# First attention on unscaled rows: turned as they land, RMS roots at read-out, first weight slab in halves on GpSimd

## The chip, the cores and the metric

The kernel runs on one core of a Trainium2 chip, in one launch. The metric is the device time of that core in microseconds (us), the median of repeated runs of the whole kernel; lower is better. The engines are named as the profile names them: PE (TensorE, matrix products; PEld is its weight load), DVE (VectorE), ACT (ScalarE), POOL (GpSimd) and SP (SyncE, which only issues transfers here).

## The reference

A sequence of 256 positions with model width 1024, batch 1, in float32, passes through two transformer blocks and then a third with another design. Only the first attention matters for the change:

```python
h = rms_norm(x, g[0])                 # x * rsqrt(mean(x*x) + EPS) * g
qkv = (h @ w_qkv)                     # 1024 -> 3 * 1024
q = q * NA_HEAD_DIM ** -0.5           # 16 heads of 64
# every position sees all 4 rows of the 4 x 64 grid, 16 columns wide, with a bias table rpb
a = softmax(q k^T + bias)
m = (a v) @ w_o
x = x + rms_norm(m, g[1])
f = conv_glu_ffn(rms_norm(x, g[2]), ...)   # and so on: FFN, gated projection, second attention ...
```

The root rsqrt(mean(x*x) + EPS) is one number per position. It multiplies a whole row of `h`, and therefore a whole row of `h @ w_qkv`; it can be put in before the product or behind it.

## The kernel before

The phases run in the order of `PHASES`: first attention (`na`), FFN, gated projection, second attention, FFN, gated projection, then the last block. Each engine has one hand-written program; the programs meet through semaphores only, so the order of calls in each program is the order of the work.

**Exact products in three passes.** Every float32 operand is split into a high part (rounded to the PE's fast format) and a low part (the operand minus its high part). A product is three matmuls: high by high, high by low, low by high (`product3`). For weights this is a pipeline over slabs of 1 MB (128 x 2048): SP's transfer into `raw` (3 buffers; slab n is issued once the low part of slab n-3 is done), ACT's `feed` copies the high part into `w_hi` (L693), DVE's `feed` subtracts for `w_lo` (L1261), PE waits in `slab(n)` for the low part. For activations `tile_parts` does the same in 8 steps per half of the positions: ACT writes `hT_hi` (L712), DVE `hT_lo` (L1283), and the two take turns.

**The start.** SP issues x in two halves of 128 positions, then slabs 0, 1 and 2. ACT sums the squares of x (`pre(0, t)`, L709), POOL turns them into roots (`powers`, L562 and L567), DVE multiplies x by them (`normed`, L1300), PE transposes the scaled rows (`turn_x`, L2003), and ACT and DVE split them. POOL makes the high part of slab 0 in one cast (L588), DVE its low part. `keep_busy` issues matmuls with no use between these steps. DVE also computes the rotary angles and the lambda sums (`lambdas`, `rotary`, L1873 to L1897) once, after slab 1. Then PE computes the first four column tiles of q and k: `first_columns` for tiles 0 and 1 (high weights against both parts, L2115, then low weights, L2120), `half_columns` for tiles 2 and 3; `turn_taps` transposes small constants (L2022 to L2028).

**The first attention.** 16 column tiles c0 to c15 (128 columns of q or k each), four value pieces, eight units of two heads. Results of PE go through four PSUM banks (`WORK = 4`) in the fixed order of `BANK_ORDER`; group g may be opened only when group g-4 has been read out (`open_bank`, `evacuated`). The order begins

```python
"c0 c1 c2 c3 taps v0.0 v0.1 T0 c4 V0 T1 c5 V1 c6 c7 v1.0 v1.1 T2 V2 T3 c8 V3 ..."   # T takes two banks
```

so c5 goes into the bank that c4 leaves. ACT reads the column tiles out (`columns_out`, L838) into `qT` and `kT`, and the values (`values_out`). The DVE's program around c4 is

```python
expand(3); feed(b + 6); feed(b + 7); output(0); output(1); feed(b + 8); feed(b + 9)
```

where feed(b+6) and feed(b+7) are the low parts of slabs 5 and 6. ACT's is `values_out(0, 0, 0)`, `values_out(0, 0, 1)`, `feed(b + 7)` (high parts of slabs 5 and 6), `columns_out(0, 4)`. PE's is value rows, `half_columns(0, 4)`, `unit_values(0, 0)`, `unit_turn(0, 1)`, `half_columns(0, 5)`.

## Time and profile before

| | us |
|---|---|
| median of 3 runs (lowest, highest) | 1225.22 (1225.15, 1225.36) |
| span of the profiled execution | 1226.3 |
| PE busy | 1210.3 (99%) |
| DVE busy | 945.3 (77%) |
| ACT busy | 672.6 (55%) |
| POOL busy | 138.0 (11%) |
| DMA | 214.52 MB, mean 175 GB/s |

The profiled execution is 1.1 us longer than the median of the unprofiled runs; differences are worked out inside the profile and then set against the median. A busy share says how long an engine had something in it, not that it worked at its peak. The chain that ended last is followed back from the last instruction to whatever released each step, so it names the engine that set the time at each moment.

### The profile page before, as it was taken

To read this page: it belongs to the slowest core of one execution; us is meant where nothing else is said; L and a number is where in the kernel's file an instruction comes from. 1 tells how busy PE (TensorE), PEld (TensorE's weight loads), DVE (VectorE), ACT (ScalarE), POOL (GpSimd) and SP (SyncE) were. 2 spreads that over 40 slices of the span, in tenths; PEclk is the share of its full clock that TensorE was granted. 3 is DMA by queue.
4 is the path that set the end of the run, shared out by engine and by line. 5 is a ranking of instruction groups with operands and counts; after the bars stand their busy time and mean duration, and the time that the engine had idled before them with its cause. 6 is when DMAs were issued, how large, how long until landed. Compare 5 with 4: busy or idle time off the path is not lost.

```text
span 1226.3 us, 17906 instructions
## 1 busy us (share of the span) xinstructions
PE 1210.3 (99%) x6995; PEld 1054.3 (86%) x6995; DVE 945.3 (77%) x1270; ACT 672.6 (55%) x1064; POOL 138.0 (11%) x257
## 2 busy tenths in 40 slices
PE   8999999999999999999999999999999999999997
PEld 7899888888879988888888988888896888888886
DVE  6757699888876588998888898776775778667665
ACT  6656644444575777444446845444675555443435
POOL 4000330000120012000002100000208420000002
PEclk9999999999999999999999999999999999999999
DMA  8834376565445445665554576555455136665540
GB/s 265 245 126 153 105 248 212 185 206 194 151 155 172 138 149 178 213 205 177 178 198 160 188 229 198 187 181 178 146 172 172 36 114 222 206 199 180 199 144 35
DMA packets 149015, 214.52 MB, mean 175 GB/s; under 512 B 4410, under 2 KB 114428, under 8 KB 148932
## 3 DMA queue, kind: packets, MB, share of 16 engines
q1 hardware_dynamic: 145596, 205.39, 51.0%
q0 software_dynamic: 1632, 4.71, 1.5%
q10 hardware_dynamic: 1704, 3.28, 0.8%
q8 instruction: 56, 0.92, 0.3%
q14 instruction: 27, 0.22, 0.1%
HBM read 212.30 MB, written 1.06 MB: 174 GB/s over the span
## 4 chain that ended last, share of the span: by engine, by line
PE 90%; DVE 5%; ACT 2%; DMA 1%; issue 1%; POOL 0%; POOLq 0%; ACTq 0%; DVEq 0%
PE work L2347 24%; PE work L2350 12%; PE acc L1946 10%; PE acc L1947 10%; PE acc L1948 10%; PE work L1946 5%; PE work L1947 5%; PE work L1948 5%; DVE w_lo L1261 2%; PE work L2156 2%; PE work L1968 2%; PE acc L2132 1%; PE work L2336 1%; PE work L2324 1%; PE work L2338 1%; PE work L2461 1%
## 5 line engine op out<-in xcount | busy, mean ns | idle before, releaser
L1261 DVE TENSOR_TENSOR w_lo<-raw,w_hi 128x2048 fp32r<-128x2048 f32 (+1 forms) x194 | 440.4, 2277 | 47.9 <-ACT w_hi L693 47.9
L693 ACT ACTIVATE w_hi<-raw 128x2048 fp32r<-128x2048 f32 (+2 forms) x193 | 365.2, 1899 | 69.3 <-PE work L2350 59.2
L2347 PE MATMUL work<-hT_both,w_hi 128*128 128x512 f32 x1280 | 318.8, 391 | 0.0
L2347 PEld LDWEIGHTS work<-hT_both,w_hi 128*128 128x128 f32 x1280 | 234.8, 188 | 45.1
L2350 PEld LDWEIGHTS work<-hT_both,w_lo 128*128 128x128 f32 x1280 | 174.6, 190 | 12.5
L2350 PE MATMUL work<-hT_both,w_lo 128*128 128x256 f32 x1280 | 178.5, 282 | 0.0
L1946 PE MATMUL acc<-w_hi,aux_hi 128*128 128x512 f32 x400 | 157.9, 395 | 0.0
L1947 PE MATMUL acc<-w_lo,aux_hi 128*128 128x512 f32 x400 | 156.7, 392 | 0.0
L1948 PE MATMUL acc<-w_hi,aux_lo 128*128 128x512 f32 x400 | 155.8, 390 | 0.0
L1048 ACT ACTIVATE aux_hi<-Z 128x256 fp32r<-128x256 f32 x88 | 36.9, 419 | 195.1 <-DVE Z L1671 107.1
L1642 DVE TENSOR_REDUCE Z<-work 128x256 f32<-128x512 f32 x88 | 60.6, 689 | 89.6 <-PE work L2350 87.8
L1948 PEld LDWEIGHTS acc<-w_hi,aux_lo 128*128 128x128 f32 x400 | 75.1, 188 | 16.4
L1946 PEld LDWEIGHTS acc<-w_hi,aux_hi 128*128 128x128 f32 x400 | 75.4, 189 | 13.8 <-issue 0.3
L1947 PEld LDWEIGHTS acc<-w_lo,aux_hi 128*128 128x128 f32 x400 | 75.5, 189 | 12.1
L562 POOL TENSOR_SCALAR ms<-ssq 128x1 f32<-128x1 f32 x26 | 19.3, 744 | 551.3 <-ACT xn L709 444.8
L1946 PE MATMUL work<-hT_both,w_hi 128*128 128x256 f32 x272 | 78.6, 289 | 0.0
L1947 PE MATMUL work<-hT_both,w_hi 128*128 128x256 f32 x272 | 76.9, 283 | 0.0
L1948 PE MATMUL work<-hT_both,w_lo 128*128 128x256 f32 x272 | 76.9, 283 | 0.0
L838 ACT ACTIVATE Z<-work 128x512 f32<-128x512 f32 (+1 forms) x92 | 45.4, 515 | 47.3 <-PE work L1948 35.9
L1946 PE MATMUL acc<-w_hi,hT_both 128*128 128x512 f32 (+1 forms) x184 | 67.8, 368 | 0.6 <-DVE hT_both L1283 0.6
L1948 PE MATMUL acc<-w_hi,hT_both 128*128 128x512 f32 (+1 forms) x184 | 66.7, 362 | 0.0
L1947 PE MATMUL acc<-w_lo,hT_both 128*128 128x512 f32 (+1 forms) x184 | 66.6, 362 | 0.0
(262 smaller groups left out, 1815.4 us busy)
## 6 DMA issues: line engine op xcount, KB each, us to landing
raw<-in_ffn_w_in SPq DMA_DIRECT2D x44, 1024.0 KB, 5.1
raw<-in_ffn_w_out SPq DMA_DIRECT2D x22, 1024.0 KB, 5.1
raw<-in_w_gate SPq DMA_DIRECT2D x22, 1024.0 KB, 5.4
raw<-in_w_up SPq DMA_DIRECT2D x22, 1024.0 KB, 5.3
raw<-in_w_down SPq DMA_DIRECT2D x22, 1024.0 KB, 5.0
raw<-in_na_w_qkv SPq DMA_DIRECT2D x12, 1024.0 KB, 7.5
raw<-in_da_w_qkv SPq DMA_DIRECT2D x12, 1024.0 KB, 5.1
raw<-in_ple_w_gate SPq DMA_DIRECT2D x8, 1024.0 KB, 5.1
```

The costliest lines, as they stand in the source:

```text
L693: act.activation(w_hi[:, n % RING, 0:size], raw[:, n % RAW, 0:size], ACT.Copy).then_inc(hi_done, 1)
L838: act.activation(dst, src, func).then_inc(bank_free[g % WORK], 1)
L1048: act.activation(aux_hi[:, c % 2, :], hid32[:, c % 2, :], ACT.Copy).then_inc(hid_hi_done, 1)
L1261: dve.tensor_tensor(w_lo[:, n % RING, 0:size], raw[:, n % RAW, 0:size], w_hi[:, n % RING, 0:size].bitcast(F32), ALU.subtract).then_inc(lo_ ...
L1642: dve.tensor_reduce(src, bank(g).rearrange("p (e s) -> p s e", e=2), AX.X, ALU.add)\
L1946: pe.matmul(dst, stationary[0], moving[0], start=first, stop=False)
L1947: pe.matmul(dst, stationary[0], moving[1], start=False, stop=False)
L1948: return pe.matmul(dst, stationary[1], moving[0], start=False, stop=last)
L1968: ins = pe.transpose(b[0:width, i * P:i * P + rows], v, ident[0:rows, 0:rows])
L2156: ins = pe.matmul(b[:, (2 * j + a) * n:(2 * j + a + 1) * n], wt[:, cols(2 * k + a)], vtok[:, k, c0:c0 + n], start=k == 0, stop=k == 1)
L2347: pe.matmul(b.rearrange("p (e s) -> p e s", e=2), v[0][:, k, cols(c % 2)], hT_both[:, k, :, :], start=k == 0, stop=False)
L2350: ins = pe.matmul(b[:, 0:S], v[1][:, k, cols(c % 2)], hT_hi[:, k, :], start=False, stop=k == KT - 1)
```

## The change

Before, the rows of x were scaled by their roots ahead of the transposition. After it, the raw rows are transposed as they land, the split and the products of the first attention run on unscaled rows, and the roots come in when PE's results are read. For that they are needed as a row across the free dimension for q and k, which are transposed: PE transposes the roots (`turn_scales(0)`), ACT copies them to `rb0`, and DVE multiplies each column tile with it (`column_scaled`). The values have positions on the partitions, and ACT scales them on the way out. All 16 column read-outs move from ACT to DVE. Slab 0 comes in two transfers, and POOL makes its high and its low part by halves; DVE has nothing more to do with slab 0. The roots are computed behind that on POOL, and behind the transfer of the bias table (`load_rpb`). Rotary work goes ahead of slab 1's low part on DVE. `first_columns` now takes slabs 0 and 1, with high weights for both tiles first. `turn_taps` goes ahead of the first scores, and fewer matmuls keep PE busy. The copy of `gb` is issued later.

```diff
-UNSCALED = [1, 4, 6, 7, 8]
+UNSCALED = [0, 1, 4, 6, 7, 8]
+SCALED_OUT = [1, 4]
         def turned_block(ph, t, step):
+            if ph == 0:
+                return acc[:, step // 4 * 2 + step % 2, step % 4 // 2 * P:(step % 4 // 2 + 1) * P]
+                if n == 0:
+                    sp.dma_start(dst[:, 0:4, :], src[:, 0:4, :]).then_inc(first_half, 16)
+                    sp.dma_start(dst[:, 4:8, :], src[:, 4:8, :]).then_inc(landed[0], 16)
             late_rows(pool)
-            powers("pre0.1")
-            pool.wait_ge(landed[0], 16)
-            pool.tensor_copy(w_hi[:, 0, :], raw[:, 0, :]).then_inc(hi_done, 1)
             for i in range(32):
                 ins = pool.memset(invf[:, i:i + 1], ...)
-            pool.wait_ge(hi_done, 2)
+            pool.wait_ge(first_half, 16)
+            pool.tensor_copy(w_hi[:, 0, first], raw[:, 0, first]).then_inc(first_hi, 1)
+            pool.wait_ge(landed[0], 16)
+            pool.tensor_copy(w_hi[:, 0, second], raw[:, 0, second]).then_inc(hi_done, 1)
+            pool.tensor_tensor(w_lo[:, 0, first], raw[:, 0, first], w_hi[:, 0, first].bitcast(F32), ALU.subtract)
+            pool.tensor_tensor(w_lo[:, 0, second], raw[:, 0, second], w_hi[:, 0, second].bitcast(F32), ALU.subtract)\
+                .then_inc(lo_done, 1)
             load_rpb(0)
+            powers("pre0.1")
@@ ACT, start
-            for t in range(T):
-                pre(0, t)
-            gains(w["norm_g"][0, 1], D)
+            pre(0, 0, (0,))
             evacuated(act, G["vec"])
             tile_parts(0, 0)
             tile_parts(0, 1)
+            pre(0, 0, (1,))
+            pre(0, 1)
             act.wait_ge(hi_done, 1)
             fed[0] = 1
             feed(3)
-            columns_out(0, 0)
-            columns_out(0, 1)
+            scales_out(0)
@@ ACT, attention0: every columns_out(0, n) is gone; values_out has scale=rstd; gains before feed(b + 11)
@@ DVE
+            def column_scaled(n):
+                g, f = G[f"c0.{n}"], n // 4 * 2 + n % 2
+                if n == 0:
+                    dve.wait_ge(scales_ready, UNSCALED.index(0) + 1)
+                full(dve, g)
+                src, roots = [v.rearrange("p (t c) -> p t c", t=T) for v in (bank(g)[:, 0:S], rb0)]
+                dst = (kT if n // 2 % 2 else qT)[:, f, :].rearrange("p (t c) -> p t c", t=T)
+                dve.tensor_tensor(dst if n // 2 % 2 else backwards(dst), src, roots, ALU.mult)\
+                    .then_inc(bank_free[g % WORK], 1)
             def attention0():
                 b = B[0]
+                column_scaled(0)
+                column_scaled(1)
                 feed(b + 3)
+                column_scaled(2)
+                column_scaled(3)
+                taps_out()
                 expand(0)
                 scores(0, 0)
                 expand(1)
-                taps_out()
                 feed(b + 4)
...
                 feed(b + 6)
                 feed(b + 7)
+                column_scaled(4)
                 output(0)
+                feed(b + 8)
+                column_scaled(5)
                 output(1)
-                feed(b + 8)
                 feed(b + 9)
+                column_scaled(6)
+                column_scaled(7)
...
@@ DVE, start
-            tile_parts(0, 0, range(4))
-            normed(0, 1)
-            tile_parts(0, 0, range(4, 8))
+            tile_parts(0, 0)
             tile_parts(0, 1)
-            feed(2)
             lambdas()
             rotary()
+            dve.wait_ge(lo_done, 1)
+            fed[0] = 1
+            feed(2)
@@ PE
+            def first_columns(n):
...
+                for k in range(KT):
+                    if n == 0:
+                        split_done(pe, 0, 1, k)
+                        if k == 0:
+                            pe.wait_ge(first_hi, 1)
+                        if k == 4:
+                            pe.wait_ge(hi_done, 1)
+                    for c in range(2):
+                        pe.matmul(b[c], hi[:, k, cols(c)], hT_hi[:, k, :], start=k == 0, stop=False)
+                        pe.matmul(b[c], hi[:, k, cols(c)], hT_lo[:, k, :], start=False, stop=False)
...
             def attention0():
-                first_columns()
-                half_columns(0, 2)
-                half_columns(0, 3)
+                first_columns(0)
+                turn_scales(0)
+                first_columns(1)
+                turn_taps()
                 unit_scores(0, 0)
-                turn_taps()
-            keep_busy(10)
+            keep_busy(2)
             pe.wait_ge(first_row, 16)
             turn(G["vec"], [vrow[0:KT, :]])
-            keep_busy(5)
+            keep_busy(4)
             turn_x(0, 0)
-            keep_busy(8)
                         turn_x(0, 1)
-                        keep_busy(2)
+                        keep_busy(6)
                         attention0()
```

## Rows read from the trace of the kernel before

**Rows 1.** The page: busy time and instructions of each engine.

```profile
PE 1210.3 (99%) x6995; PEld 1054.3 (86%) x6995; DVE 945.3 (77%) x1270; ACT 672.6 (55%) x1064; POOL 138.0 (11%) x257
```

**Rows 2.** Windows; columns: stretch, length, PE, PEld, DVE, ACT, POOL busy, PEclk, DMA.

```profile
27.30:40.00 12.70, 12.68 (x67) 9.93 (x68) 11.79 (x17) 7.93 (x19) 0.00 (x0) 1.00 0.78 249
```

**Rows 3.** The chain that ended last, first 28 us: start, length, what.

```profile
0.80 3.64 DMA x<-in_x
...
14.56 0.38 ACT hT_both L712
...
15.35 0.38 ACT hT_both L712
...
16.36 4.40 DVE w_lo L1261 x2
```

**Rows 4.** Timeline of PE, 1.5 to 29.1 us: start, length, engine, line, operation.

```profile
1.58 4.38 PE L2015 MATMUL work<-ident 128*128 128x128 f32 x20 [1.58 <-POOL ident L544]
5.89 0.22 PE L1968 MATMUL work<-ident,Z 8*128 8x8 f32 x1
6.04 1.38 PE L2015 MATMUL work<-ident 128*128 128x128 f32 x10
...
18.66 2.13 PE L2120 MATMUL work<-hT_both,w_lo 128*128 128x256 f32 x16
...
26.55 0.28 PE L1948 MATMUL work<-hT_both,w_lo 128*128 128x256 f32 x1
27.32 0.49 PE L2132 MATMUL acc<-Z 64*128 64x256 f32 x2 [0.50 <-ACT Z L838]
```

**Rows 5.** Timeline of POOL, first 20 us, and POOL's subtraction elsewhere, by line.

```profile
9.61 1.89 POOL L588 CAST w_hi<-raw 128x2048 fp32r<-128x2048 f32 x1 [0.99 <-DMA raw<-in_na_w_qkv]
...
18.08 1.51 POOL L579 DMA_DIRECT2D Z<-in_na_rpb  x2 [5.31 <-ACT w_hi L693]
...
L644 POOL TENSOR_TENSOR Z<-Z x7: 1893/1935/2016, 920.3 to 970.8; 128x1024 f32<-128x1024 f32 x6, 128x512 f32<-128x512 f32 x1
```

**Rows 6.** Timeline of POOL after 300 us: a root alone, and one beside DVE.

```profile
323.06 2.35 POOL L565 TENSOR_SCALAR ms<-ssq 128x1 f32<-128x1 f32 x1 [154.85 <-ACT Z L709]
...
341.19 0.22 POOL L562 TENSOR_SCALAR ms<-ssq 128x1 f32<-128x1 f32 x1
...
341.88 0.57 POOL L567 TENSOR_TENSOR rstd<-ms,mhalf 128x1 f32<-128x1 f32 x1
```

**Rows 7.** DVE: the scaling of x by its line (min/median/max ns), then timeline lines.

```profile
L1300 DVE TENSOR_SCALAR xn<-x,rstd x4: 474/484/1725, 6.9 to 11.7; 128x512 f32<-128x512 f32 x4
...
9.79 0.35 DVE L1283 SCALAR_TENSOR_TENSOR hT_both<-acc,vecT,hT_both 128x128 fp32r<-128x128 f32 x1
10.05 1.73 DVE L1300 TENSOR_SCALAR xn<-x,rstd 128x512 f32<-128x512 f32 x1
...
20.67 0.32 DVE L1873 TENSOR_TENSOR Z<-Z 128x128 f32<-128x128 f32 x1
...
24.96 2.29 DVE L1261 TENSOR_TENSOR w_lo<-raw,w_hi 128x2048 fp32r<-128x2048 f32 x1
...
27.97 0.96 DVE L1448 TENSOR_TENSOR Z<-Z 128x768 f32<-128x768 f32 x1 [0.72 <-DMA Z<-in_na_rpb]
...
320.87 4.49 DVE L1261 TENSOR_TENSOR w_lo<-raw,w_hi 128x2048 fp32r<-128x2048 f32 x2
```

**Rows 8.** Around column tile 4: timelines of ACT and DVE, and PE's chain.

```profile
42.46 0.60 ACT L838 ACTIVATE Z<-work 128x512 f32<-128x512 f32 x1 [0.90 <-PE work L1948]
42.95 3.70 ACT L693 ACTIVATE w_hi<-raw 128x2048 fp32r<-128x2048 f32 x2
...
44.89 4.50 DVE L1261 TENSOR_TENSOR w_lo<-raw,w_hi 128x2048 fp32r<-128x2048 f32 x2 [2.96 <-ACT w_hi L693]
49.51 0.42 DVE L1488 TENSOR_TENSOR xn<-work,rinv 128x256 f32<-128x256 f32 x1
...
47.91 0.12 PE work L1946
```

## What the change should do, worked out before it ran

> **What bounds the kernel now.** I read the page first: PE is busy for 1210.3 us [rows 1] of the span of 1226.3. So what counts is the 16 us that PE lacks, and, at the start, the time in which it is only kept busy. The windows say where that ends: from 27.3 us on PE is full (12.68 of 12.70 us) [rows 2]. The change only touches what comes ahead of that and the queues of the first attention, up to some 125 us. The chain gives the order of the start [rows 3]: x lands at 4.44; the splits run in pairs, 14.56 to 15.35, so 0.79 us for two steps, to 16.36; then come the low parts of slabs 0 and 1, 4.40. In between, from 10.05, DVE scaled the second half of x, the first piece in 1.73 us [rows 7]. PE's own timeline [rows 4] has the low products of slab 0 at 18.66, tiles 2 and 3 behind them, from 20.8 until the last starts at 26.55 (48 matmuls, 5.87 us, 0.122 each) and the first scores at 27.32. With 1.06 for eight score matmuls and 0.7 for the taps behind them, the value products start at 29.1. That moment is what I carry: everything behind it is packed, so its shift is the gain, unless a new hole appears later.
>
> **The change: the start.** *Removed*: four scalings of x, the root from the path to the split, DVE's 2.2 us for slab 0. *The split* now starts when the gains and the first four raw blocks are turned. The gains' row is in by 5.89 at the latest, because PE turned it then, only just out of its filler [rows 4]; how much earlier, no row tells, but x itself lands at 4.44 [rows 3]. With four fillers (8 records at 0.12 to 0.22 each, 1.0 to 1.7 us) and four blocks (0.5 to 0.9) the first split stands between 6 and 8.5; I take 6.8, nearer the early end since x's transfer, 128 times larger, took only 3.6. Sixteen splits at 0.395 and a tail of 0.3 end at 13.4, against 16.36. *Slab 0 on POOL*: it lands at 9.55 (the cast started at 9.61 behind it), and the cast of 2048 columns took 1.89, so a half 0.95 [rows 5]; the first half is done before, the second at 10.6. Two subtractions of 1024 columns at 1.94 each [rows 5] end at 14.5, against some 18.5 on DVE. PE's high products keep step with the splits (four matmuls, 0.49, per step of 0.395) and end near 14; the 16 low ones take 2.1 [rows 4] and end near 16.7, against 20.8. That looks like 4 us, but PE then waits for the roots.
>
> **Roots are next in line.** On POOL, behind slab 0, come the two issues of the bias table, 1.5 us [rows 5], so 16.0. A root with all its sums there takes 1.26 (from 341.19 to 342.45) [rows 6], two take 2.6: 18.6. ACT's squares are no later: the splits end for ACT at 13.1, three squares at 0.66 end at 15.1. ACT then makes the high parts of slabs 1 and 2, 1.9 each, until 18.9; DVE does 4.3 us of lambdas and rotary (20.67 to 24.96 [rows 7]) from 13.4 or, if it has to stand behind POOL's second subtraction, from 14.5, so until 17.7 to 18.8, then the low part of slab 1, 2.28, until at most 21.1. So PE: two small transposes, 0.3, to 18.9; tiles 2 and 3, 5.87, to 24.8 (the low part of slab 1 is wanted at 22.8 and there); taps 0.7 to 25.5; scores 1.06 to 26.6. The taps ahead of the scores cover the read-out of tile 3 (0.35). Values start at 26.6 against 29.1: **2.5 us earlier**.
>
> **What must keep up.** The bias table landed just under 27.97, from an issue at 18.08 [rows 5, 7]: 9.9 us. Issued at 14.5 it lands near 24.4, and DVE wants it at 26.2: hidden with 1.8 to spare. Slab 3 is issued with it and its low part is done at about 32.9, against a need at 33.1: a slack of some 0.3, as before. The late `gb`, the sums, `values_out` with a scale and the split transfer I cost at nothing: ACT drops 16 read-outs of 0.37 and has room, and SP is idle from 11 to 18 us; were that cover gone, an issue is 0.4.
>
> **The first attention: a new hole.** Sixteen read-outs go to DVE. The nearest row is its product of a 128x256 PSUM tile, 0.42 [rows 8]; I take 0.35 each as the next instruction starts 0.34 later, 5.6 us together. The place matters more than the sum. Tile 5 uses tile 4's bank. PE opened the bank at 47.91 without a wait, since ACT had read tile 4 right behind its high parts of slabs 5 and 6, which end at 46.65 [rows 8]. Now DVE reads it behind the low parts of slabs 5 and 6, and these hang on ACT's high parts, which start when the second value piece, full at 42.42, has been read. Counted from there all of it moves with PE: subtractions until +7.0 (44.89 + 4.50), tile 4 read at +7.3, PE wants the bank at +5.5. So PE stands still for **1.8 us** (1.7 to 1.9), once. The other places hold: tile 5 is read at +10.7, its bank wanted at +17; tile 8 at 80.8 against 85.6; tile 12 at 94.4 against 100.9; tile 14 at 101.1 against 105.4 (before's clock, in all of them the next value comes from the same kind of count). DVE's seventh scores come 0.7 later, with 2 us before anybody needs them.
>
> **Sum.** -2.5 + 1.8 = -0.7 inside the profile (1226.3 to 1225.6); from the median 1225.22 this gives 1224.6.
>
> **A rule against the trace.** DVE's scaling of x, 0.48 in the median, took 1.73 beside POOL's cast [rows 5, 7], while a split from PSUM beside the same cast kept its 0.35 [rows 7]. And a one-column instruction of POOL took 2.35 at 323.06, where DVE was in its low part until 325.3 [rows 6, 7]. The Trainium skill (SBUF — State Buffer, section on SBUF's two separate sides) says that DVE and GpSimd share one port pair, which a DVE instruction with two SBUF inputs holds against a GpSimd instruction that reads SBUF, for its whole length. The trace agrees in these places. By that rule the splits from PSUM don't suffer from POOL's subtractions, but lambdas and rotary must stand behind the second one.
>
> **Rivals.**
> 1. *The root behind DVE's low part (slower).* If DVE starts slab 1's low part before POOL has started its last power, at 18.0, POOL waits for 2.3 us as in rows 6. Then the roots come at 20.9, values start only 0.2 us early, and with the hole the sum is +1.6: 1226.8. Its point: DVE must be through with rotary before 18.0. For: splits done at 13.4 plus 4.3 is 17.7. Against: POOL's subtraction until 14.5 stops DVE first, as it was stopped at 10.05, and gives 18.8. This is a matter of tenths.
> 2. *No hole at tile 5.* If PE reaches tile 5 later than I count, or DVE's part ends early, 2.5 us stay: 1222.7. Against: the order is fixed in both programs, and all terms are rows.
> 3. *PE at half speed.* Its first 20 records come 0.22 apart, the ten from 6.04 on 0.13 [rows 4], as 1.2 against 2.4 GHz, though the granted clock reads 1.00. It had been busy for 4 us without a pause. The new start is filled less. If it is slow at 10.7, four matmuls take 0.86 a step and the first products end between 17.5 and 19.5: up to 0.9 late, 1225.5; if it falls back in the wait of 2 us for the roots, tiles 2 and 3 lose 1.5 more: up to 1227.
> 4. *Roots not late.* Should POOL be quicker than the rows of other shapes say, by 0.5 per subtraction, it is 1223.6.
>
> **How the numbers follow.** Forecast, the sum as it stands: 45% (1223.9 to 1225.6). Rival 1: 25%. Rival 2: 10%. Rival 3: 12%. Rival 4: 8%. The likeliest gives 1224.6. Two tenths of a per cent, which is about what a measurement of this kernel can tell from no change, are 2.45 us, so faster means under 1222.8, slower over 1227.7. Under 1222.8 is rival 2 in half of its cases and a sum of 4 with good luck: 9%. Over 1227.7 are rivals 1 and 3 together, or a slab that comes late in the thin slack of 0.3: 11%. Same: 80%. The range runs from rival 2's 1222.7 to rivals 1 and 3 with half of their extras, 1227.5.
>
> **What would show it.** In the profile after: the first split near 6.8 and the last near 13.4; POOL's subtractions 1.9 each, low part of slab 0 by 14.5; the second root near 18.6 with no POOL instruction of over 2 us (rival 1 has one, beside a 2.3 us subtraction on DVE); tiles 2 and 3 from 19 to 24.8 at 0.122 a matmul (rival 3: over 0.2); value products from 26.6; one wait of PE of 1.8 us ahead of tile 5, released by DVE's read-out of tile 4, and no other up to 125 us. I would be wrong if POOL's work on slab 0 runs much slower beside DVE's splits, or if the bias table or slab 3 lands later than the same distance behind its issue.

## The result: 8 us slower

The median went from 1225.36 us (1225.15 to 1225.55, five runs) to 1233.37 (1232.10 to 1233.57, five runs). The ratio is 1.0063, with a 95% interval of 1.0053 to 1.0074. The forecast was 1224.6, and the measured time lies outside the range up to 1227.5.

The profile page of the changed kernel, busy time and instructions of each engine, and the granted clock in 40 slices:

```profile
span 1231.6 us, 17868 instructions
PE 1209.7 (98%) x6971; PEld 1054.1 (86%) x6971; DVE 949.7 (77%) x1281; ACT 668.6 (54%) x1049; POOL 144.8 (12%) x260
PEclk8999999999999999999999999999999999999999
```

PE's busy time is 0.6 us less than in [rows 1], while the span is 5.3 us longer: PE does not do more, it waits more. (The span in [rows 1] is that of an execution that was itself some 2.7 us longer than the usual one: executions of 1225.3 us have a span of 1223.6, and the 1.1 us in the text on the kernel before sets a span against a time. Where most of them arise comes below.)

**Where the time arises.** A mark that both kernels have is PE's transposition of x ahead of each later phase. First the kernel before, then the changed one: count, min/median/max in ns, first and last start.

```profile
L2003 PE MATMUL acc<-ident,x x80: 270/272/329, 137.8 to 1007.6; 128*128 128x128 f32 x80
...
L2003 PE MATMUL acc<-ident,x x16: 272/272/273, 872.4 to 878.2; 128*128 128x128 f32 x16
```

```profile
L2048 PE MATMUL acc<-ident,x x80: 270/272/328, 145.5 to 1013.0; 128*128 128x128 f32 x80
...
L2048 PE MATMUL acc<-ident,x x16: 270/272/273, 880.0 to 885.9; 128*128 128x128 f32 x16
```

The first of these marks is 7.7 us later, the one at 880 is 7.6 later, the last 5.4. So all of the loss arises ahead of 138 us, in the start and the first attention, and nothing is won or lost for 730 us behind it. The 2.2 us that seem to come back at the end belong to the profiled execution of the kernel before. Windows, columns as in [rows 2], before and then changed:

```profile
940.00:1000.00 60.00, 58.57 (x355) 50.74 (x356) 44.01 (x63) 29.80 (x57) 22.80 (x18) 0.97 0.21 63
```

```profile
940.00:1000.00 60.00, 58.22 (x361) 49.61 (x360) 42.70 (x65) 32.22 (x67) 29.35 (x25) 1.00 0.22 71
```

The clock of 0.97 over 60 us is a stretch of some 3.4 us at half clock, in that one execution, which costs at most 1.7 us; a wait of PE for ACT in the same stretch is 1.2 us instead of 0.7. Together these are the 2.2 us. So the marks, not the spans, give the effect.

**The start.** POOL's timeline of the changed kernel, with three of DVE's lines among it, the last its low part of slab 1 (start, length, engine, line, operation, idle time before it and its releaser):

```profile
9.96 1.04 POOL L599 CAST w_hi<-raw 128x1024 fp32r<-128x1024 f32 x1 [3.60 <-DMA raw<-in_na_w_qkv]
...
12.18 1.04 POOL L601 CAST w_hi<-raw 128x1024 fp32r<-128x1024 f32 x1 [1.18 <-DMA raw<-in_na_w_qkv]
...
13.19 2.44 POOL L603 TENSOR_TENSOR w_lo<-raw,w_hi 128x1024 fp32r<-128x1024 f32 x1
...
13.60 2.06 DVE L1915 CAST posf<-posi 128x2 f32<-128x2 int32 x1
...
15.59 2.38 POOL L605 TENSOR_TENSOR w_lo<-raw,w_hi 128x1024 fp32r<-128x1024 f32 x1
...
15.69 2.98 DVE L1918 TENSOR_SCALAR Z<-Z,posf 128x32 f32<-128x32 f32 x4
...
17.92 1.47 POOL L587 DMA_DIRECT2D Z<-in_na_rpb  x2
...
21.18 2.48 POOL L570 TENSOR_SCALAR ms<-ssq,ms 128x1 f32<-128x1 f32 x1
21.31 2.28 DVE L1272 TENSOR_TENSOR w_lo<-raw,w_hi 128x2048 fp32r<-128x2048 f32 x1
23.75 0.56 POOL L575 TENSOR_TENSOR rstd<-ms,mhalf 128x1 f32<-128x1 f32 x1
```

Both halves of slab 0 land late (9.9 and 12.1; in [rows 5] the whole slab was there at 9.6), each subtraction takes 2.4, and the second root's sum is stretched from some 0.3 to 2.48 by DVE's subtraction beside it. Then PE:

```profile
24.36 0.48 PE L2055 MATMUL acc<-ident,rstd 128*128 128x128 f32 x1 [3.20 <-POOL rstd L575]
...
28.05 0.41 PE L2165 MATMUL work<-hT_both,w_hi 128*128 128x256 f32 x1
...
30.20 0.28 PE L2166 MATMUL work<-hT_both,w_hi 128*128 128x256 f32 x1
...
30.80 2.08 PE L2170 MATMUL work<-hT_both,w_lo 128*128 128x256 f32 x16
...
33.14 1.19 PE L2181 MATMUL acc<-Z 64*128 64x256 f32 x8
```

It stands for 3.2 us for the root, and the matmuls behind that are 0.41 long, and 0.213 apart, until 29.8, when they go back to 0.28 and 0.12 apart. The windows give the granted clock (the third column from the end, 1.00 being 2.4 GHz): 0.51 between 25 and 30 us is the 1.2 GHz level. It fell while PE stood still, 1.00 from 22 to 23 us and 0.55 from 23 to 24.

```profile
20.00:25.00 5.00, 1.17 (x6) 0.77 (x6) 3.46 (x6) 0.12 (x1) 4.35 (x8) 0.81 1.05 308
25.00:30.00 5.00, 5.00 (x26) 5.00 (x25) 2.95 (x3) 4.94 (x6) 3.89 (x8) 0.51 1.06 268
```

The first scores start at 33.14 against 27.32 [rows 4], the value products at 34.3 against 29.1: 5.2 of the 7.7 us. **Tile 5** adds the next piece; ACT, DVE and PE around it, the lines that answer to [rows 8]:

```profile
48.24 3.70 ACT L708 ACTIVATE w_hi<-raw 128x2048 fp32r<-128x2048 f32 x2
...
50.17 4.49 DVE L1272 TENSOR_TENSOR w_lo<-raw,w_hi 128x2048 fp32r<-128x2048 f32 x2 [2.96 <-ACT w_hi L708]
54.59 0.41 DVE L1530 TENSOR_TENSOR Z<-work,pts 128x256 f32<-128x256 f32 x1
...
55.15 0.36 PE L1982 MATMUL work<-hT_both,w_hi 128*128 128x256 f32 x1 [2.05 <-DVE Z L1530]
```

PE waits for 2.05 us, and tile 5 starts at 55.15 against 47.91 [rows 8], 7.24 later (5.2 + 2.05). The last 0.45 us up to the first mark come from small gaps behind it.

### The profile page after: what moved, and what is told of

It reads as the page before. It is cut to its first block, busy times and chain, and to the rows that moved or that the text cites. A ratio compares the mean times of both kernels' runs of the same rounds, so it can differ in the third digit from the quotient of the medians.

```text
span 1231.6 us, 17868 instructions
## 1 busy us (share of the span) xinstructions
PE 1209.7 (98%) x6971; PEld 1054.1 (86%) x6971; DVE 949.7 (77%) x1281; ACT 668.6 (54%) x1049; POOL 144.8 (12%) x260
## 4 chain that ended last, share of the span: by engine, by line
PE 90%; DVE 4%; ACT 2%; DMA 1%; POOL 1%; issue 1%; SPq 0%; POOLq 0%; ACTq 0%; DVEq 0%
PE work L2396 24%; PE work L2399 12%; PE acc L1982 10%; PE acc L1983 10%; PE acc L1984 9%; PE work L1982 5%; PE work L1983 4%; PE work L1984 4%; DVE w_lo L1272 2%; PE work L2205 2%; PE work L2004 1%; PE acc L2181 1%; PE work L2385 1%; PE work L2373 1%; PE work L2387 1%; PE work L2510 1%
## 5 line engine op out<-in xcount | busy, mean ns | idle before, releaser
L1272 DVE TENSOR_TENSOR w_lo<-raw,w_hi 128x2048 fp32r<-128x2048 f32 (+2 forms) x193 | 438.0, 2275 | 46.7 <-ACT w_hi L708 46.6
L2399 PEld LDWEIGHTS work<-hT_both,w_lo 128*128 128x128 f32 x1280 | 174.6, 190 | 12.5
L2399 PE MATMUL work<-hT_both,w_lo 128*128 128x256 f32 x1280 | 178.5, 282 | 0.0
L1679 DVE TENSOR_REDUCE Z<-work 128x256 f32<-128x512 f32 x88 | 60.6, 688 | 90.6 <-PE work L2399 88.8
L1983 PEld LDWEIGHTS acc<-w_lo,aux_hi 128*128 128x128 f32 x400 | 75.5, 189 | 12.1
L1982 PE MATMUL work<-hT_both,w_hi 128*128 128x256 f32 x256 | 74.0, 289 | 2.1 <-DVE Z L1530 2.1
L1983 PE MATMUL work<-hT_both,w_hi 128*128 128x256 f32 x256 | 72.4, 283 | 0.0
L1984 PE MATMUL work<-hT_both,w_lo 128*128 128x256 f32 x256 | 72.3, 283 | 0.0
L1704 DVE TENSOR_REDUCE Z<-work 128x256 f32<-128x512 f32 x88 | 60.1, 683 | 2.8 <-PE work L2399 2.8
```

The source lines that it names most:

```text
L1272: dve.tensor_tensor(w_lo[:, n % RING, 0:size], raw[:, n % RAW, 0:size], w_hi[:, n % RING, 0:size].bitcast(F32), ALU.subtract).then_inc(lo_ ...
L1679: dve.tensor_reduce(src, bank(g).rearrange("p (e s) -> p s e", e=2), AX.X, ALU.add)\
L1704: dve.tensor_reduce(hid, bank(g + 1).rearrange("p (e s) -> p s e", e=2), AX.X, ALU.add)\
L1982: pe.matmul(dst, stationary[0], moving[0], start=first, stop=False)
L1983: pe.matmul(dst, stationary[0], moving[1], start=False, stop=False)
L1984: return pe.matmul(dst, stationary[1], moving[0], start=False, stop=last)
```

## The experiments

The kernels that ran together share their runs of the kernel before (median 1225.25 beside the first four, 1225.38 beside the next four, 1225.71 beside the two after that, 1225.33 beside the last two). Brackets hold the 95% interval of the ratio. The last four kernels ran on another chip than the first eight, so each is to be compared with the kernel before of its own group.

### One suspect at a time

**Tile 4 read ahead of the second slab.** Is the wait at tile 5 worth its 2 us?

```diff
@@ DVE, attention0
                 feed(b + 6)
-                feed(b + 7)
                 column_scaled(4)
+                feed(b + 7)
                 output(0)
```

> The changed kernel with DVE's read-out of column tile 4 put between the low parts of slabs 5 and 6 instead of behind both. Theory H (the hole at tile 5 is a cost of its own): PE's wait of 2.05 us ahead of tile 5 goes, since the read-out comes 2.2 us sooner, and the time falls by 1.9 to 2.1, from 1233.4 to about 1231.4. Rival (the time is set further on by slabs that land late, so a wait removed here comes back at tiles 6 to 8): the wait at tile 5 goes, another of 1 us or more appears before 80 us, and the time falls by under 1.0.

Measured: 1233.18 us, ratio 1.0061 [1.0046, 1.0076]: 0.2 less than the changed kernel. The wait at tile 5 is gone, but another of the same length stands ahead of the third unit's scores (PE's waits: in total, times, longest; then DVE's timeline):

```profile
PE acc L2181 <- issue: 2.1, 1, 2.1
```

```profile
61.58 2.29 DVE L1272 TENSOR_TENSOR w_lo<-raw,w_hi 128x2048 fp32r<-128x2048 f32 x1 [4.07 <-ACT w_hi L708]
63.79 0.75 DVE L1530 TENSOR_TENSOR Z<-work,pts 128x256 f32<-128x256 f32 x2
```

The third unit needs tile 6, which DVE reads only behind the low part of slab 8, and that slab's high part waited 5.3 us for its transfer. The hole at tile 5 covered a second one behind it. The clock has a share in this, too. Behind the new wait it is 0.57 from 64 to 68 us, while the first fall, in the wait for the root, was shorter in this execution and let the scores start at 31.8 instead of 33.14, though that wait was 3.2 us as before. Wait and clock together cancel out: the first mark stands at 145.4 against 145.5. A step that I costed by itself was worth nothing by itself.

**The three small transfers later.** The changed ACT program no longer computes squares first, so lambda's 128 KB and the positions and the small table (1 KB each, in pieces of 4 bytes) are issued at 1.4 to 3.1 us, beside x and slab 0. This puts them back behind a piece of squares:

```diff
@@ ACT, start
-            act.dma_start(z(11864, 12120), ... w["da_lambda"] ...).then_inc(lam_loaded, 16)
-                act.dma_start(posi[:, :], ...).then_inc(pos_loaded, 16)
-                act.dma_start(tT[:, :], ...).then_inc(t5_loaded, 16)
             pre(0, 0, (0,))
+            act.dma_start(z(11864, 12120), ...)
+                act.dma_start(posi[:, :], ...)
+                act.dma_start(tT[:, :], ...)
             evacuated(act, G["vec"])
```

> The changed kernel with ACT's three small transfers (lambda, positions, table: 128 KB and two of 1 KB in 4-byte pieces) issued behind its first sum of squares, near 5.5 us, as they stood in the kernel before (5.8), instead of ahead of it (1.4 to 3.1). Theory T (these transfers, moved ahead of slab 0, are what delays it): the first half of slab 0 lands at 8.0 or sooner instead of 9.9 and the second at 9.6 to 10.2 instead of 12.1, POOL's low part of slab 0 ends some 2 us sooner than 18.0, and the roots come earlier. Rival S (the split of slab 0's transfer into two is what delays it): the landings stay at 9.9 and 12.1 within 0.4. For the total time theory T expects 1 to 3 us less, unless the second root is again held behind a subtraction of DVE, in which case under 1.

Measured: 1228.03 us, 1.0028 [1.0016, 1.0039]: 5.4 us less, two thirds of the loss, for three moved issues. The windows from 5 to 7.5 us (last column GB/s) of the changed kernel, of this one, and POOL's timeline of this one:

```profile
5.00:7.50 2.50, 2.27 (x11) 1.87 (x10) 0.51 (x2) 1.21 (x5) 1.36 (x33) 1.00 0.87 212
```

```profile
5.00:7.50 2.50, 1.71 (x9) 1.31 (x7) 0.61 (x2) 1.09 (x5) 1.36 (x33) 1.00 1.04 355
```

```profile
7.83 1.04 POOL L599 CAST w_hi<-raw 128x1024 fp32r<-128x1024 f32 x1 [1.48 <-DMA raw<-in_na_w_qkv]
9.35 1.04 POOL L601 CAST w_hi<-raw 128x1024 fp32r<-128x1024 f32 x1 [0.48 <-DMA raw<-in_na_w_qkv]
10.35 2.37 POOL L603 TENSOR_TENSOR w_lo<-raw,w_hi 128x1024 fp32r<-128x1024 f32 x1
...
18.35 0.31 POOL L570 TENSOR_SCALAR ms<-ssq,ms 128x1 f32<-128x1 f32 x1
```

The halves land 2.1 and 2.8 us sooner. The second root's sum now takes 0.31, because it comes before DVE's subtraction (at 18.93), PE hardly stands for the roots, and the clock stays at 1.00 from 20 to 30 us: the scores start at 26.2, 6.9 sooner. So this one cause carried two others. Part of it goes again at tile 5, where the wait remains and the clock now falls behind it:

```profile
48.73 0.40 PE L1982 MATMUL work<-hT_both,w_hi 128*128 128x256 f32 x1 [2.05 <-DVE Z L1530]
```

```profile
48.00:50.00 2.00, 1.27 (x7) 1.30 (x7) 1.84 (x5) 1.23 (x1) 0.00 (x0) 0.73 1.02 193
50.00:52.00 2.00, 2.00 (x11) 2.00 (x11) 1.55 (x1) 0.00 (x0) 0.00 (x0) 0.50 1.09 336
```

**Both roots ahead of slab 1's low part**: the collision alone, with slab 0 still late.

```diff
@@ DVE, start
             dve.wait_ge(lo_done, 1)
+            dve.wait_ge(rstd_done, 2)
             fed[0] = 1
             feed(2)
```

> The changed kernel with one wait more: DVE starts the low part of slab 1 only when both roots are there. Theory C (POOL's second root is held by DVE's subtraction through the port they share): POOL's second sum takes 0.3 instead of 2.48 us, the second root is there at 22.1 instead of 24.3, tiles 2 and 3 start 2.2 us sooner, and with a wait of PE that is 2.2 shorter the clock may not fall at all: 2 us less if it still falls, 4 to 5 less if it doesn't. Rival (the 2.48 is a slow instruction of POOL's own): it stays over 2 us and the time is the same or later by what DVE now waits.

Measured: 1230.16 us, 1.0038 [1.0023, 1.0053]: 3.2 us less. POOL and DVE:

```profile
21.63 0.36 POOL L570 TENSOR_SCALAR ms<-ssq,ms 128x1 f32<-128x1 f32 x1
...
22.73 2.29 DVE L1272 TENSOR_TENSOR w_lo<-raw,w_hi 128x2048 fp32r<-128x2048 f32 x1 [0.88 <-POOL rstd L575]
```

The same instruction, at nearly the same time of the kernel, takes 0.36 instead of 2.48 once DVE's subtraction stands behind it. The longest wait of PE for a root is 1.1 instead of 3.2, the granted clock is 1.00 from 20 to 30 us, and the scores start at 29.0. Making DVE wait 0.9 us for POOL made the kernel faster. I had expected 4 to 5 us less if the clock did not fall. It did not fall here, but behind the wait of 2.05 at tile 5 it did, to 0.57 from 52 to 56 us, as in the second run.

**PE kept warm**: the clock alone, with filler matmuls in the wait for the roots.

```diff
@@ PE, attention0
                 first_columns(0)
+                keep_busy(16)
                 turn_scales(0)
```

> The changed kernel with 16 more filler matmuls (32 records, some 3.8 us) between the low products of slab 0 and the transposes of the roots. Theory K (the clock at half speed from 24 to 30 us is a cost of its own, caused by the wait for the second root): the granted clock stays at 1.00 from 20 to 30 us, the 32 high products of tiles 2 and 3 take 3.8 us instead of 6.4, and the time falls by 2.2 to 2.6. Rival (what is saved here is waited for at the low part of slab 2 or at the scores): the clock stays up, but the value products start less than 1 us sooner than at 34.3.

Measured: 1232.05 us, 1.0051 [1.0036, 1.0066], the profiled execution 1230.71: 1.3 to 2.7 less. The clock no longer falls:

```profile
20.00:30.00 10.00, 9.53 (x82) 9.28 (x81) 6.85 (x11) 5.11 (x6) 8.19 (x15) 1.00 1.05 268
```

The scores start at 30.8, 2.3 sooner than without the filler, and the roots as late as ever. So the fall of the clock costs 2.3 us at that place, of which the time gives back 1.3 in the median. The profiled execution was the fastest of the four; why the others gave back less is not shown.

### The cause of the late slab

Two runs ask whether it was really the moved transfers, and not the cut into halves.

**The kernel before, with the three issues ahead of the squares:**

```diff
@@ before.py, ACT, start
+            act.dma_start(z(11864, 12120), ...)
+                act.dma_start(posi[:, :], ...)
+                act.dma_start(tT[:, :], ...)
             for t in range(T):
                 pre(0, t)
-            act.dma_start(z(11864, 12120), ...)
-                act.dma_start(posi[:, :], ...)
-                act.dma_start(tT[:, :], ...)
```

> The kernel before with one edit: ACT's three small transfers (lambda, positions, table) are issued ahead of its sums of squares, near 1.4 us, as in the changed kernel. Theory T (their pieces hold up what is queued behind them on the same DMA engines): slab 0, whole, lands 1.5 to 2.6 us later than 9.55, and the rate falls to under 300 GB/s somewhere between 5 and 8 us. In time little, since here slab 0 is wanted at 13.8 only: within 1 us of before. Rival (the delay in the changed kernel is of its two half transfers): slab 0 still lands at 9.6 within 0.4.

Measured: 1225.90 us, 1.0003 [0.9994, 1.0012]. The rate and POOL's cast:

```profile
5.00:7.50 2.50, 1.87 (x15) 1.54 (x13) 0.60 (x3) 2.26 (x8) 1.68 (x5) 1.00 0.81 209
```

```profile
11.92 1.89 POOL L588 CAST w_hi<-raw 128x2048 fp32r<-128x2048 f32 x1 [3.17 <-DMA raw<-in_na_w_qkv]
```

The slab is late by 2.3 us in the old kernel too (11.92 against 9.61 [rows 5]), at 209 GB/s where it had 344. But the time hardly changes. PE waits 1.6 us for the cast and starts on slab 0 at 13.87, where it started at 13.88 before: DVE's scaling of the second half of x no longer meets the cast (0.88 us for both pieces, 2.12 before), and so the splits end 1.1 us sooner. In the changed kernel there is no such scaling, and nothing gives the late slab back.

**The changed kernel with slab 0 in one transfer:**

```diff
@@ SP, slabs
-                if n == 0:
-                    sp.dma_start(dst[:, 0:4, :], src[:, 0:4, :]).then_inc(first_half, 16)
-                    sp.dma_start(dst[:, 4:8, :], src[:, 4:8, :]).then_inc(landed[0], 16)
-                else:
-                    sp.dma_start(dst, src).then_inc(landed[n % RAW], 16)
+                sp.dma_start(dst, src).then_inc(landed[n % RAW], 16)
@@ POOL
-            pool.wait_ge(first_half, 16)
+            pool.wait_ge(landed[0], 16)
```

> The changed kernel with slab 0 in one transfer again; POOL waits for the whole before its first cast. Theory T (small transfers delay the slab, the halves don't): the slab lands at 12.1 within 0.4, where the second half did; both casts come behind it, so the low part ends 1.0 later than 18.0, and the time is 0.5 to 1.5 more than 1233.4. Rival S (two issues and two completions cost the delay): it lands near 10 and the time falls by 1 us or more.

Measured: 1234.40 us, 1.0071 [1.0055, 1.0086], 1.0 more than in halves. The slab lands when its second half did:

```profile
12.04 1.04 POOL L595 CAST w_hi<-raw 128x1024 fp32r<-128x1024 f32 x1 [5.68 <-DMA raw<-in_na_w_qkv]
```

The halves are not the cause; they bring the low part 0.9 us sooner (17.97 against 18.83). That is not what the time shows, though: the clock's first fall was shorter here, the scores start at 32.8, 0.3 us sooner than in halves, and the time is lost behind tile 5, where the clock is 0.50 from 56 to 58 us. The cause of the late slab is settled: the same three issues, moved in either kernel, move slab 0 by over 2 us. All other profiles agree. With the three issues early, the second half or the whole slab is there at 11.9 to 12.7 us in all six kernels; with them later, at 9.0 to 9.6 in all eight.

### All mended, and what stands behind it

**All four places mended**: the transfers as in the second run, the roots as in the third, tile 4 as in the first, and tile 6 ahead of the low part of slab 8.

```diff
@@ DVE, attention0, with the three edits above
                 output(1)
-                feed(b + 9)
                 column_scaled(6)
+                feed(b + 9)
                 column_scaled(7)
```

> The changed kernel with three things mended: ACT's small transfers behind its first sum of squares, DVE's low part of slab 1 behind both roots, and tiles 4 and 6 read out one low part sooner each (tile 4 between slabs 5 and 6, tile 6 ahead of slab 8). Theory (the loss is made of separate costs, each with its place): against the run with the transfers alone (1228.0) the wait at tile 5 goes, 2.0 us, and with it the stretch at half clock that followed at 49 to 53 us, 1.5 to 1.9 us: 1224.1 to 1224.6, so 0.7 to 1.2 below the kernel before, since its scores start 1.1 sooner. Rival (a bound further on, the bias table's landing at 27.8 and the slabs behind it, takes the gain): over 1226.

Measured: 1224.88 us (1223.52 to 1225.73, eleven runs), 0.9992 [0.9983, 1.0001]: 8.5 us less than the changed kernel, and no difference from the kernel before that could be measured. The scores start at 25.6, 1.7 us ahead of [rows 4]. The value products, the moment that the prediction carried, start at 26.69 against 29.1, so 2.4 us ahead where 2.5 was forecast. Of that 1.3 is lost by 35 us, and at the first mark 0.7 is left (137.1 against 137.8). The first value product, DVE's timeline, and the one wait of PE of over 0.3 us:

```profile
26.69 0.50 PE L1983 MATMUL work<-w_hi,hT_both 128*128 128x512 f32 x1
```

```profile
28.27 0.96 DVE L1459 TENSOR_TENSOR Z<-Z 128x768 f32<-128x768 f32 x1 [1.42 <-DMA Z<-in_na_rpb]
...
32.66 2.29 DVE L1272 TENSOR_TENSOR w_lo<-raw,w_hi 128x2048 fp32r<-128x2048 f32 x1
```

```profile
PE work L1983 <- DVE w_lo L1272: 1.3, 1, 1.3
```

The bias table lands at 28.25, no sooner than before [rows 7], though it was issued 3 us sooner, and the low part of slab 3 stands behind it on DVE.

**The same without tile 6**, to price that one move:

```diff
@@ DVE, attention0, against the run above
-                column_scaled(6)
                 feed(b + 9)
+                column_scaled(6)
```

> As the run with everything mended, but of the read-outs only that of tile 4 is moved; tile 6 is still read behind the low part of slab 8. Theory (the first read-out only passes the wait on to the next one, since slab 8 lands late): no wait at tile 5, one of about 2 us ahead of the scores of the third unit, near 58 us, with the clock falling behind it, and 3 to 4 us more than the run with both moved. Rival (tile 6 costs nothing in this start): within 0.5 us of it.

Measured: 1226.98 us, 1.0013 [1.0004, 1.0022]: 2.1 more in the median, where I had expected 3 to 4. The wait is there, of 1.4, but the clock stays at 1.00 behind it. The profiled execution was the fastest of the ten, 1225.74, so this wait need not be that of the median:

```profile
PE acc L2182 <- issue: 1.4, 1, 1.4
```

**Slab 3's low part ahead of the bias table.** If DVE's order is the last thing in the way, this should win, by 1.6 to 2.0 us over the kernel before.

```diff
@@ DVE, attention0, all mended
                 taps_out()
+                feed(b + 4)
                 expand(0)
                 scores(0, 0)
                 expand(1)
-                feed(b + 4)
```

> The run with everything mended, and DVE's low part of slab 3 put ahead of the bias work and the first scores. Theory B (once the roots are early, the bias table's landing at 28.2 us sets the next wait: DVE stands 1.42 us for it with slab 3 behind it in its queue, and PE waits 1.3 us for slab 3's low part): DVE does slab 3 while it would stand idle, PE's wait of 1.3 us goes, and the time falls from 1224.9 to 1223.4 to 1223.8, 1.6 to 2.0 under the kernel before. Rival (the first exponents come 1.2 us later and PE waits for them instead): a wait for ACT ahead of the first weight transposes near 38 us, and the time stays within 0.4 of 1224.9.

Measured: 1227.07 us (1223.60 to 1229.98, eleven runs), 1.0006 [0.9996, 1.0016]. The profiled execution was the fastest one, a span of 1221.8 without any wait of PE of over 0.3 us between 18 and 125 us; the others were up to 6.4 us slower. Its first mark stands at 135.8, 2.0 us ahead of the kernel before. I first took the start's clock for the reason of the spread, since it stood at half for some 3 us there.

**The bias table issued ahead of slab 0's work:**

```diff
@@ POOL, start, all mended
+            load_rpb(0)
             pool.wait_ge(first_half, 16)
...
-            load_rpb(0)
             powers("pre0.1")
```

> The run with everything mended, and POOL issues the bias table's two transfers ahead of its first cast of slab 0 (near 6.4 us) instead of behind its subtractions (14.9). Theory B: the table lands before 25 us, DVE no longer waits for it, PE's wait of 1.3 us goes; but its 0.9 MB run among slabs 0 to 2, so slab 0 lands 0.5 to 2 us later and the roots with it: 1223.5 to 1226. Rival (the table's landing is bound by its own queue's pace, not by its start): it still lands after 27 us and the time is no better than 1224.9.

Measured: 1226.65 us, 1.0006 [0.9997, 1.0015]. Nobody waits for the bias table any more; issued at 6.3 us, it lands near 20. But slab 1 is now late, by 4.9 us:

```profile
19.52 1.91 ACT L708 ACTIVATE w_hi<-raw 128x2048 fp32r<-128x2048 f32 x1 [4.99 <-DMA raw<-in_na_w_qkv]
```

PE waits 2.2 us for it. Here what came in sooner pushed out what was to come.

**Slab 3 first, with more filler in PE**, and **slab 3 first once more**, side by side on one chip, to see whether the spread is the clock's.

```diff
@@ PE, start, slab 3 first
-            keep_busy(2)
+            keep_busy(6)
             pe.wait_ge(first_row, 16)
...
+                        keep_busy(6)
                         turn_x(0, 1)
```

> The mended kernel with slab 3 first, and more filler matmuls: 6 instead of 2 at the very start and 6 between the transposes of the first and of the second half of x, so that PE has fewer gaps ahead of 13 us, where that kernel's profile had it at half clock (10.6 to 14 us). That kernel's eleven executions lay between 1223.6 and 1230.0. Theory K (the spread is the clock, which falls in some executions and not in others): the granted clock stays at 1.00 to 60 us, the executions lie within 2 us of each other and the median near the best of the other, 1223.4 to 1224.2. Rival (the spread comes from when the slabs land): the clock stays up, but the executions spread as before, over 3 us.

> The mended kernel with slab 3 first once more, unchanged, beside the one with more fillers on the same chip, since its first executions spread over 6 us and only the fastest was profiled. Theory K: it spreads by 3 us or more again and its median lies 1 us or more above the filled one. Rival: both spread alike and their medians agree within 0.7 us.

Measured: 1225.28 us, 0.9999 [0.9990, 1.0008], with filler; 1225.89, 1.0006 [0.9996, 1.0016], without. They spread from 1223.9 to 1227.8 with it and from 1223.5 to 1228.8 without, so the filler does not remove the spread. ACT's high part of slab 3 says what does differ between executions; first the fastest one, above, then the one again, of 1227.2 us, then the filled one, of 1226.9:

```profile
24.68 1.91 ACT L708 ACTIVATE w_hi<-raw 128x2048 fp32r<-128x2048 f32 x1 [1.53 <-DMA raw<-in_na_w_qkv]
```

```profile
28.44 1.92 ACT L708 ACTIVATE w_hi<-raw 128x2048 fp32r<-128x2048 f32 x1 [5.10 <-DMA raw<-in_na_w_qkv]
```

```profile
28.27 1.92 ACT L708 ACTIVATE w_hi<-raw 128x2048 fp32r<-128x2048 f32 x1 [5.09 <-DMA raw<-in_na_w_qkv]
```

In one execution slab 3 is there at 24.7, in the others at 28.3 to 28.4, and in both late ones PE waits 2.0 us for ACT's read-out of the values and 1.1 or 1.2 in all for its exponentials, which stand behind the high part of slab 3 on ACT. Three profiled executions show this together, and in those of the second run, of all four places mended and of the same without tile 6 the slab is there at 25.0 to 25.4. Why it lands at one time or the other is not settled. It was under way in the same stretch as the bias table, which fits but was not tried by itself. Nor is it known whether the spread belongs to this order of DVE's work: the kernel with all four places mended, which spread by 2.2 us, was not run on this chip, and the one with the bias table sooner spread by 3.4 here. No version beats the kernel before beyond what can be measured.

## Why the prediction was wrong

The step that failed first is the landing of slab 0, put at 9.55 where it was 12.1: the removed squares were costed as free time of ACT, not as cover for the transfers behind them. By its own steps:

- **The splits: right.** The first stands at 6.5 (forecast 6.8), the last ends at 13.1 (13.4). That the splits from PSUM keep their pace beside POOL's subtractions can't be seen here, as the first subtraction starts at 13.19, behind the last split; the second run shows it, with 0.61 for two splits while POOL subtracted. That rotary work stands behind POOL's subtractions came true: a conversion of two columns took 2.06 us, until the first one's end. Not all did: a reduction of 0.29 us at 13.39 ran beside it unhindered.
- **Slab 0 lands at 9.55: wrong, and the largest error.** Its second half landed at 12.1. I took its landing from [rows 5] and costed the removed squares at ACT only as freed time. But ACT also issues transfers, and without the squares ahead of them these went out at 1.4 to 3.1 us. That a moved step also moves the transfers issued behind it is what I left out: worth 5.4 us by the second run, since two other costs hang on it, the root beside DVE and the clock.
- **A subtraction of 1024 columns on POOL, 1.94: too small.** It took 2.36 to 2.44, in every run, whatever DVE did. The row was of a subtraction of the same width in another place and form; two of them make 0.9 us. The casts were right (1.04 against 0.95), and so was the issue of the bias table (1.47 against 1.5).
- **Roots at 18.6: wrong.** They came at 24.3, 5.7 later: 2.6 for the landing, 0.9 for the subtractions, 2.2 for **rival 1**, which happened as described: a one-column instruction of 2.48 beside DVE's 2.28. I gave it 25%, from a count in which DVE reached its subtraction at 17.7 to 18.8 and the roots were through at 18.0. Both sides of that race hang on one event, the end of POOL's second subtraction, here at 17.97: DVE's rotary steps stood beside the subtractions (2.06 and 2.98 us), and from there DVE needed 3.3 us to its own subtraction and POOL 3.2 to the second root's sum. (DVE's wait for `lo_done` had long been over.) With slab 0 whole it was 3.1 against 3.3, and the sum took 2.31. In the second run it was 3.9 against 3.3, since there the subtraction also held DVE's product for lambda, for 2.31 us, and the root came first. So it was a matter of tenths, as I had written, but not of the moments of 17.7 and 18.0: with the slab in time the root wins by 0.6 us, and the late slab turned it.
- **Rival 3, half speed behind a wait: happened,** at the second of the places that I had named. I priced it at 1.5; it cost 2.3 to 2.4 (tiles 2 and 3 took 8.2 us instead of 5.87), since 24 of their 48 matmuls ran at the lower level. The wait ahead of it was 3.2 and not 2, but that this is the reason is not shown: in the first run a wait of 3.2 was followed by only 11.
- **The hole at tile 5: right** in place, cause and size (2.05 against 1.8). What I missed is that it hid a second one at tile 6, behind slab 8: so the term was right in the sum, and wrong as a statement of what its removal would bring.
- **The bias table lands 9.9 us behind its issue: wrong.** It was ready at 27.6 to 28.3 in the kernels with the three transfers later, issued at 14.9 or 15.0, and just under 27.97 in the kernel before, issued at 18.08 [rows 5, 7]: 12.5 to 13.4 us against 9.9. A landing is not its issue plus a constant. Had the start come out as forecast, some 1.3 us would have been lost here, an estimate from PE's wait with all four places mended, where the start was as forecast to 0.1 us.
- **The sum.** The value products were to start 2.5 us early and started 5.2 late. The difference of 7.7 is the roots (5.6 at PE), the clock (2.4), less 0.3 for taps and scores. With 2.05 and 0.45 behind them the marks move by 7.7, and the medians by 8.0.
- **The range.** Rivals 1 and 3 were taken as cases side by side, with half of their extras together at the upper end. They are links of a chain: late slab, so a root beside DVE, so a long wait, so the lower clock; in the second and third run the links behind the one that was mended went with it. For that reason alone the range should have reached to their full sum with the hole, by my own prices 1226.8 + 2.4 = 1229.2. The late landing (2.6) and POOL's subtractions (0.9), at which I had put no upper bound, are most of the 4.2 us from there to what was measured.

Could the idea have won? With all four places mended the value products start 2.4 us ahead, against the 2.5 that I worked out, and most of this goes to the next bound: the bias table, which lands at 28.25 as before, and the low part of slab 3, which stands behind it in DVE's program. With slab 3 first, the one profiled execution without a wait kept 2.0 us of it. The gain is there in the start, but no version brought it to the end in the median.

## What to carry to other kernels

When work is taken off an engine's program, list the issues of transfers that stood behind it: they go out sooner, and small ones beside a large one that somebody waits for delayed it here by more than 2 us. Ask of each rival whether it has the same cause as another, and if it has, price them in series. Before removing work from the start of a kernel, look for the transfers that land just ahead of the moment when the bounding engine fills up: they are what the gain will run into. Issuing one sooner may not help: here 3 us sooner brought the bias table no sooner than before, and issued at 6.3 us it came early and slab 1 4.9 us late.

## What the runs showed of the hardware

- Three transfers, of 128 KB and twice 1 KB in 4-byte pieces, issued at 1.4 to 3.1 us, lowered the rate in the window from 5 to 7.5 us from 344 or 355 to 209 or 212 GB/s, in one pair of profiles of either kernel. In all six kernels with the early issues it was 194 to 240, in all eight without them 344 to 367. Which of the three does it wasn't tried.
- A POOL subtraction of 128 x 1024 float32 takes 2.36 to 2.44 us where its cast to the high part takes 1.04 and another subtraction of the same width took 1.94 [rows 5].
- A one-column POOL instruction of 0.3 us takes 2.48 when it meets a DVE subtraction of 2.28 with both operands in SBUF. The Trainium skill (SBUF — State Buffer, section on SBUF's two separate sides) states that between such a DVE instruction and a GpSimd one that reads SBUF the first to start has their shared port pair for its whole length, and the other is blocked. The length agrees, and so does the third run, with 0.36 for the same instruction without the neighbour. Who started first is not clear from the records: POOL's starts 0.13 us before DVE's here and 0.12 us behind it with slab 0 whole, and was held both times.
- PE's clock was at 1.2 GHz for 5.3 us behind a wait of 3.2 us, from 24.5 to 29.8; behind the same wait in the first run it was back at 2.4 GHz near 27. Behind the wait of 2.05 at tile 5 it fell in the second run (0.50 from 50 to 52 us), in the third and with slab 0 whole, but neither in the run kept warm nor in the changed kernel:

```profile
40.00:60.00 20.00, 17.95 (x128) 16.55 (x127) 15.32 (x15) 12.48 (x18) 1.46 (x2) 1.00 0.81 227
```

  The waits are equal, so their length alone doesn't decide it; what does stays open.
- The landing of a 1 MB slab differed by 3.7 us (24.7 and 28.4) between two executions of one program, and the time of that program spread by 5 to 6 us, where the kernel before spread by 0.7 to 2.3 beside it.
